# Four weight streams of the mixing layers in three rounded passes, the token shift made while leaving PSUM

## The reference, cut to what matters

```python
for l in range(DEPTH):                       # two mixing layers
    h = _rms_norm(x, norm_pre[l]) * (1 + scale[:, None, :]) + shift[:, None, :]
    p = h @ w_in[l]                          # 256 tokens x 1024, times 1024 x N_IN
...
# RWKV-7 branch: streams holds r, k, v (1024 wide each) and two narrow ones
prev = jnp.pad(streams, ((0, 0), (1, 0), (0, 0)))[:, :-1]
streams = streams + mu * (prev - streams)    # the token shift
r, k, v, w_l, a_l = _split(streams, ...)
w = -jax.nn.softplus(-(w0 + jnp.tanh(w_l) @ w2)) - 0.5
decay = jnp.exp(-jnp.exp(w))
a = jax.nn.sigmoid(a0 + a_l @ a2)
kk = heads(k * k_k)
kk = kk / jnp.maximum(jnp.sqrt(jnp.sum(kk * kk, -1, keepdims=True)), 1e-12)
k = k * (1 + (a - 1) * k_a)
...                                          # state over the tokens, in chunks of 64 here
y = (y - mean) * lax.rsqrt(var + RWKV_GN_EPS)
y = y * ln_w + ln_b
bonus = jnp.sum(r_h * k_h * r_k, -1, keepdims=True) * v_h
o_rwkv = ((y + bonus) * jax.nn.silu(z)) @ w_o
# GLA branch: q, k (512 wide each), v, a gate, z
log_a = jax.nn.log_sigmoid(g_l @ w2 + g_bias) / GLA_GATE_NORM
```

## Time and profile before

| | us |
|---|---|
| median of three runs (2013.95 to 2016.42) | 2014.83 |
| the profiled execution | 2014.74 |
| its span, first to last instruction | 2013.0 |
| TensorE busy | 1929.2 (96%) |
| VectorE busy | 1328.2 (66%) |
| ScalarE busy | 713.8 (35%) |

### The profile page before, as it was taken

How to read it: one execution, slowest core, us unless ns; L and a number is a source line. 1 busy time by engine, 2 the same in 40 slices (tenths; PEclk the granted TensorE clock), 3 DMA queues, 4 the chain that set the end, 5 groups by cost and what they waited for, 6 DMA issues and landing times.

```text
span 2013.0 us, 41616 instructions
## 1 busy us (share of the span) xinstructions
PE 1929.2 (96%) x18047; PEld 1783.3 (89%) x18047; DVE 1328.2 (66%) x1722; ACT 713.8 (35%) x1023; POOL 97.7 (5%) x137
## 2 busy tenths in 40 slices
PE   8999999999899999999999999997999998999998
PEld 8988999998599999989887879996998887888997
DVE  7896687747657866864675339676764676428765
ACT  5573433435533331240423123243222234204243
POOL 2000000100400000020000000001002000000000
PEclk9999999999999998999999999998999999999999
DMA  8555478853347794645440236454653540135643
GB/s 216 140 144 157 149 236 266 266 147 116 99 148 258 253 258 106 166 117 154 118 116 6 74 102 173 122 161 104 170 160 102 148 128 22 45 99 147 164 121 111
DMA packets 473063, 291.41 MB, mean 145 GB/s; under 512 B 26679, under 2 KB 467484, under 8 KB 472776
## 3 DMA queue, kind: packets, MB, share of 16 engines
q1 hardware_dynamic: 466688, 262.20, 46.7%
q0 software_dynamic: 5312, 25.32, 3.3%
q10 hardware_dynamic: 904, 1.58, 0.3%
HBM read 288.02 MB, written 1.05 MB: 144 GB/s over the span
## 4 chain that ended last, share of the span: by engine, by line
PE 82%; DVE 13%; ACT 3%; issue 2%; POOL 0%; DMA 0%; DVEq 0%; ACTq 0%; POOLq 0%
PE bank L705 38%; PE bank L1422 6%; PE bank L1424 6%; PE bank L1423 6%; PE bank L694 4%; PE bank L664 2%; DVE rounded L730 2%; PE bank L901 2%; PE bank L893 2%; PE bank L1625 1%; PE bank L1612 1%; PE bank L1068 1%; PE bank L787 1%; PE bank L1474 1%; PE bank L1593 1%
## 5 line engine op out<-in xcount | busy, mean ns | idle before, releaser
L705 PE MATMUL bank<-rounded 128*128 128x256 f32 (+1 forms) x4584 | 564.2, 284 | 12.0 <-DVE rounded L730 9.4
L705 PEld LDWEIGHTS bank<-rounded 128*128 128x128 f32 (+1 forms) x4584 | 550.6, 189 | 21.2 <-DVE rounded L730 14.6
L730 DVE TENSOR_TENSOR rounded<-arena,rounded 128x1024 fp32r<-128x1024 f32 (+1 forms) x251 | 303.4, 1214 | 86.6 <-ACT rounded L719 80.5
L1422 PE MATMUL bank<-parts 128*128 128x256 f32 x1024 | 290.5, 284 | 1.0 <-DVE parts L2226 1.0
L1424 PE MATMUL bank<-parts 128*128 128x256 f32 x1024 | 289.8, 283 | 0.0
L1423 PE MATMUL bank<-parts 128*128 128x256 f32 x1024 | 289.8, 283 | 0.0
L705 PE MATMUL bank<-common,arena 128*128 128x256 f32 x1280 | 285.4, 380 | 0.0
L705 PEld LDWEIGHTS bank<-common,arena 128*128 128x128 f32 x1280 | 240.1, 189 | 39.8 <-issue 4.8
L770 ACT ACTIVATE arena<-bank 128x512 f32<-128x512 f32 x114 | 67.6, 597 | 436.1 <-PE bank L705 423.1
L1422 PEld LDWEIGHTS bank<-parts 128*128 128x128 f32 x1024 | 196.5, 192 | 1.5 <-issue 1.3
L1423 PEld LDWEIGHTS bank<-parts 128*128 128x128 f32 x1024 | 196.6, 192 | 0.1
(11 more groups left out here) (391 smaller groups left out, 2497.9 us busy)
## 6 DMA issues: line engine op xcount, KB each, us to landing
arena<-in_w_in SPq DMA_DIRECT2D x190, 512.0 KB, 3.8
whole<-in_ffn_w_gate_up SPq DMA_DIRECT2D x44, 1024.0 KB, 5.2
arena<-in_ada_w POOLq DMA_DIRECT2D x32, 768.0 KB, 6.3
whole<-in_ffn_w_down SPq DMA_DIRECT2D x16, 1408.0 KB, 7.0
arena<-in_rec_w_in SPq DMA_DIRECT2D x36, 512.0 KB, 3.8
arena<-in_att_w_qkv SPq DMA_DIRECT2D x24, 512.0 KB, 3.7
arena<-in_rec_w_out SPq DMA_DIRECT2D x16, 512.0 KB, 3.7
arena<-in_mla_w_o SPq DMA_DIRECT2D x16, 512.0 KB, 3.8
```

The costliest lines, as they stand in the source:

```text
L705: last = pe.matmul(psum[s][0:c, m % 2 * T:m % 2 * T + T], w[a][:, k, cols], x[b][:, k, :], start=(k, a, b) == (0, 0, 0), stop=k == job.kt ...
L730: dve.tensor_tensor(raw_view(job_of[u], u, UNIT_LOW), raw, high_view(job_of[u], u).bitcast(F32), ALU.subtract)\
L1422: pe.matmul(bank, w_hi, x_hi, start=start and k == 0, stop=False)
```

## The change

It does the following.

- r, v, gq and gk become split streams, with high parts by ScalarE (24 units in each of the two layers). The high parts of r and v lie in three new buffers, `KEY_HIGHS`; `AA` and `CC` move onto `KKDD` and `V_`, so that `HX` stays as it is until the chunks.
- The token shift of k, r and v is made in two steps. ScalarE leaves PSUM with four reads of 128 x 256 for each bank, where it made one of 128 x 512: each tile times `1 - mu` into the result, and times `mu` into the shifted buffer. VectorE adds the two (`mix_kept_v`), one addition of 2048 numbers a row in place of the subtraction and eight multiply-adds.
- `split_v` is called at eighteen more places of `rwkv_v`, `high_act` at more places of ScalarE's lists.
- The eight multiply-adds by `ln_w` and `ln_b` move from VectorE to ScalarE.
- `HX` is made again right after the last tile of the chunks, not during ro.
- TensorE makes five units of v, not four, ahead of the sums over heads of `RK`, and waits for `HX` ahead of gq, not of gv.

```diff
-        AA, SW, CC = (buf(DK, T) for _ in range(3))
+        SW = buf(DK, T)
+        assert place[0] <= lent + HIGHS * UNIT
+        AA, CC = KKDD, V_
...
-                "k": proj("k", 4, "vector"), "r": proj("r", 4), "v": proj("v", 4),
+                "k": proj("k", 4, "vector"), "r": proj("r", 4, "scalar", highs=KEY_HIGHS), "v": proj("v", 4, "scalar", highs=KEY_HIGHS),
...
-                "gq": proj("gq", 2), "gk": proj("gk", 2),
+                "gq": proj("gq", 2, "scalar"), "gk": proj("gk", 2, "scalar"),
...
-            multiply_units(j["v"], range(4))
+            multiply_units(j["v"], range(5))
             head_sums_pe(RK, DK, abanks)
-            multiply_units(j["v"], range(4, 8))
+            multiply_units(j["v"], range(5, 8))
...
-        def mix_v(src, dst, nt, mu, l):
...
+        def mix_kept_v(shifted, dst):
+
+            dve.tensor_tensor(dst, dst, shifted[:, :, 0:T], ALU.add)\
+               .then_inc(vector_step.sem, 1)
...
             tile_out_v(1)
+            dve.wait_ge(layer_high_again.sem, layer_high_again.due(dve))
+            dve.tensor_tensor(HX[1], H, HX[0].bitcast(F32), ALU.subtract)\
+               .then_inc(layer_split.sem, 1)
...
+            dve.tensor_scalar(KEPT, col(n2("rwkv_mu"), 0, 24), -1.0, 1.0, ALU.mult, ALU.add)\
...
             chunk_tiles_v()
+            split_v(j["gq"].first + 2)
...
+            split_v(j["gk"].first)
             dve.wait_ge(head_rms.sem, head_rms.due(dve))
             dve.tensor_tensor(R, R, RST, ALU.mult)\
...
+               .then_inc(heads_scaled.sem, 1)
+            dve.wait_ge(heads_scaled.sem, heads_scaled.due(dve))
+            split_v(j["gk"].first + 2)
+            dve.wait_ge(heads_shifted.sem, heads_shifted.due(dve, DK))
             dve.tensor_tensor(R, R, BONUS, ALU.add)\
...
+            split_v(j["gk"].through())
             dve.tensor_tensor(R, R, ZR, ALU.mult)\
...
+        def keep_mixed(dst, shifted, mu, l):
+
+            def step(i, bank, done, rounds):
+                for n in range(2):
+                    k = 2 * i + n
+                    act.activation(dst[:, k, :], bank[:, n, :], ACT.Copy, scale=KEPT[:, mu + k:mu + k + 1])\
+                       .then_inc(scalar_step.sem, 1)
+                    scalar_step.due(act)
+                    last = act.activation(shifted[:, k, 1:T + 1], bank[:, n, :], ACT.Copy, scale=col(f"rwkv_mu_2/{l}", mu + k))
+                last.then_inc(done, 1)
+            return step
...
-            take_units(act, j["k"], keep(raw[0], ACT.Copy, 1))
+            take_units(act, j["k"], keep_mixed(KR_, raw[0], 8, l), only=range(3))
+            high_act(j["r"].first)
+            take_units(act, j["k"], keep_mixed(KR_, raw[0], 8, l), only=range(3, 4))
+            high_act(j["r"].first + 2)
...
-            take_units(act, j["r"], keep(raw[1], ACT.Copy, 1))
+            take_units(act, j["r"], keep_mixed(R, raw[1], 0, l), high_before(j["r"], 2))
...
+            act.wait_ge(inner_summed.sem, 2 * l + 2)
+            act.activation(HX[0], H, ACT.Copy)\
+               .then_inc(layer_high_again.sem, 1)
+            high_act(j["gq"].first + 2)
+            take_units(act, j["rz2"], keep(ZR[:, 6:], ACT.Silu))
...
-            take_units(act, j["gq"], keep(GQ, ACT.Copy))
-            take_units(act, j["gk"], keep(GK, ACT.Copy), high_before(j["gk"], 4), only=range(1))
+            take_units(act, j["gq"], keep(GQ, ACT.Copy), high_before(j["gq"], 2), only=range(1))
+            high_act(j["gk"].first + 1)
+            act.wait_ge(heads_scaled.sem, heads_scaled.due(act))
+            for k in range(DK):
+                act.activation(R[:, k, :], R[:, k, :], ACT.Identity, bias=col(f"rwkv_ln_b_2/{l}", k), scale=col(f"rwkv_ln_w_2/{l}", k))\
+                   .then_inc(heads_shifted.sem, 1)
+            take_units(act, j["gq"], keep(GQ, ACT.Copy), only=range(1, 2))
+            take_units(act, j["gk"], keep(GK, ACT.Copy), high_before(j["gk"], 2), only=range(1))
             act.wait_ge(gate_in.sem, gate_in.due(act))
...
-            take_units(act, j["gk"], keep(GK, ACT.Copy), high_before(j["gk"], 3), only=range(1, 2))
+            take_units(act, j["gk"], keep(GK, ACT.Copy), high_before(j["gk"], 2), only=range(1, 2))
             high_act(j["ro"].first + 3)
```

More of the change, by code:

```diff
@@ L397, in program @@
         ECEND = buf(DK, 4)
-        KAI = buf(8)
+        KAI, KEPT = buf(8), buf(24)
         assert place[0] <= AR
         place[0] = after_preparation
+        KEY_HIGHS = [rounded(UNIT, at=aligned() + n * UNIT) for n in range(HIGHS)]
         R_HIGH = rounded(DK, T)
@@ L2778, in rwkv_v @@
             dve.wait_ge(cumulated.sem, cumulated.due(dve))
+            split_v(j["r"].first + 4)
             dve.tensor_scalar(KAI, col(n2("rwkv_k_a"), 0, 8), -1.0, 1.0, ALU.mult, ALU.add)\
@@ L2788, in rwkv_v @@
             dve.wait_ge(vector_step.sem, kfactors)
+            split_v(j["r"].first + 5)
             dve.tensor_tensor(KR_, KR_, KFACTOR, ALU.mult)\
@@ L2791, in rwkv_v @@
             dve.wait_ge(vector_step.sem, vector_step.due(dve))
+            split_v(j["v"].first)
             for k in range(0, DK, 2):
@@ L2804, in rwkv_v @@
             dve.wait_ge(vector_step.sem, vector_step.due(dve))
+            split_v(j["v"].first + 3)
             dve.tensor_tensor(RK, RK, along(col(n2("rwkv_r_k"), 0, 8), DK, T), ALU.mult)\
@@ L2807, in rwkv_v @@
             dve.wait_ge(head_squares.sem, head_squares.due(dve))
+            split_v(j["v"].first + 4)
             dve.wait_ge(head_rms.sem, head_rms.due(dve))
@@ L2811, in rwkv_v @@
             dve.wait_ge(vector_step.sem, vector_step.due(dve))
+            split_v(j["v"].first + 5)
             dve.tensor_tensor(BDF, KKD, AA, ALU.mult)\
@@ L2814, in rwkv_v @@
             dve.wait_ge(vector_step.sem, vector_step.due(dve))
+            split_v(j["v"].first + 6)
             dve.wait_ge(decays.sem, decays.due(dve))
@@ L2821, in rwkv_v @@
             dve.wait_ge(vector_step.sem, vector_step.due(dve))
+            split_v(j["v"].through())
             dve.tensor_tensor(BDF, BDF, E2, ALU.mult)\
@@ L3378, in rwkv_act @@
             act.wait_ge(scalar_step.sem, scalar_step.due(act))
+            high_act(j["v"].first + 4)
             act.activation(flat(SW), flat(SW), ACT.Exp, scale=-KAPPA)\
@@ L3381, in rwkv_act @@
             act.wait_ge(decays.sem, decays.due(act))
+            take_units(act, j["v"], keep_mixed(V_, raw[2], 16, l), only=range(1))
             act.wait_ge(guarded_squares.sem, guarded_squares.due(act))
@@ L3385, in rwkv_act @@
             act.wait_ge(scalar_step.sem, scalar_step.due(act))
+            high_act(j["v"].first + 5)
             act.activation(flat(SQR), flat(SQR), ACT.Exp, scale=-0.5)\
@@ L3388, in rwkv_act @@
             act.wait_ge(head_rms.sem, head_rms.due(act))
-            take_units(act, j["v"], keep(raw[2], ACT.Copy, 1), only=range(2))
+            take_units(act, j["v"], keep_mixed(V_, raw[2], 16, l), only=range(1, 2))
+            high_act(j["v"].first + 6)
             for k in range(0, DK, 2):
@@ L3396, in rwkv_act @@
                 act.nop().then_inc(bonus_sums.sem, 1)
-            take_units(act, j["v"], keep(raw[2], ACT.Copy, 1), only=range(2, 4))
+            high_act(j["v"].through())
+            take_units(act, j["v"], keep_mixed(V_, raw[2], 16, l), only=range(2, 4))
             act.wait_ge(taken[0].sem, halves(0, j["mo"]))
```

46 lines of the change are left out of this document (18 added, 28 removed).

## The result

The changed kernel takes **2037.05 us** (median of 4 runs, 2035.79 to 2038.55), the one before, run beside it, 2014.67. The ratio is 1.0109, 95% interval 1.0097 to 1.0122: 22 us slower, where the prediction said 30. The profiled execution has a span of 2034.0 us against 2013.0.

What follows compares the result with a forecast made beforehand. TensorE was taken to set the pace in both stretches. Added waits less savings, 0.2 + 3.0 + 12.1 = 15.3 us a layer, twice 30.6, on a median of 2014.83 gave 2045 us; range 2037 to 2050 (70%).

Steps and rivals of the forecast that it cites:

- k to r: Between k and r: ScalarE's longer bank reads and two high parts delay the gates; r begins 3.55 us later.
- lost in r: During r: TensorE waits for VectorE's low parts of units 4, 5 and 6, together 3.2 us.
- lost in v and head sums: During v: waits for low parts 1.5, sums of `RK` 1.4, unit 7 2.8; together 5.7 us.
- wait of the R sums: After the chunks: low part of `HX` and three low parts stand ahead of the head sums' signal, 0.9 us.
- gq unit 3: In gq: unit 3's high part queues on ScalarE behind the exponential of the norms; TensorE waits 2.8 us.
- waits in gk: In gk: its two last high parts follow weight and bias on ScalarE; waits of 1.4 and 0.7 us.
- pause ahead of ro: Between gk and ro: ro's first high parts stand behind the gate's exponential and logarithm; TensorE waits 10.5 us.
- ro to gv: During ro: one wait of 2.1 us, gate sums ahead of unit 2, against 1.6 before; +0.5.
- L1713 to gv: Stretch behind the chunks: waits less the saving on gq and gk sum to +12.1 us a layer.
- Rival 3: Ahead of ro and at the gates: TensorE's clock falls after new pauses, up to 2.4 us each; 2055 at most, 14%.
- Rival 2: Ahead of ro: only this wait is small, so 10.5 us a layer go; 2024 us, chance 10%.
- Rival 1: All split streams: VectorE's low parts ready in time everywhere, all 28.2 us gained; 1986.5 us, chance 6%.

Runs made afterwards that it cites:

- head: gates_first, with VectorE's low parts of r and of v's last unit also moved earlier in its list: 2024.56 us, ratio 1.0048.
- both2: head and tail, plus the gate's input made earlier in SQT's space and more of ro's parts ahead of the gate work: 1997.51 us, ratio 0.9916.
- ro_ahead: Changed kernel with ro's first two high parts and their low parts moved ahead of the gate on ScalarE and VectorE: 2039.89 us, ratio 1.0131.
- both: Changed kernel with the reorderings of head and tail together: 2016.88 us, ratio 1.0006.
- filled: Changed kernel with 16 useless matmuls put into TensorE's pause ahead of ro: 2038.51 us, ratio 1.0121.
- tail: Changed kernel with only the stretch behind the chunks reordered, some of gq's and ro's parts made earlier: 2031.80 us, ratio 1.0082.
- gates_first: Changed kernel with no high copy between k's last bank and the gates on ScalarE: 2033.75 us, ratio 1.0097.

## Why the prediction was right, and 8 us high, by its steps

First layer, us:

| step | predicted | measured |
|---|---|---|
| k to r | +3.75 (0.2 of it in k) | +3.81 |
| lost in r | 3.2 | 2.7 (listed waits 0.84, 0.96, 0.36; the rest to eight units at 2.88) |
| lost in v and head sums | 5.7 | 4.4, of it 2.7 ahead of unit 7 |
| saved on r and v | 9.4 | 9.4 |
| sum to the chunks | +3.2 | +1.6 (second layer +3.0) |
| wait of the R sums (the first head sums behind the chunks) | 0.9 | 0 (L1713 to the head sums 9.05 in both kernels) |
| gq unit 3 | 2.8 | 2.76, and 1.5 of half clock |
| waits in gk | 2.1 | 0 |
| pause ahead of ro | 10.5 | 8.8 |
| ro to gv | +0.5 | +0.3 |
| saved on gq and gk | 4.7 | 4.2, as what the other rows leave |
| L1713 to gv | +12.1 | +9.2 (second layer +8.9) |

**Right:** the sign, the places, and what ends each wait. "ro's first high parts stand behind the gate's exponential and logarithm" is the chain above, row by row; TensorE waits for VectorE's low parts in r and v, 5.6 us where the prediction said about 8, and unit 7 stands where said. One wait was not there: the head sums of `RK` run through in 3.03 us, as the others do. ScalarE came to their banks at 1016.89, not 1019.7, so the 1.4 us at the fourth bank never came.

**A sign of being wrong that showed:** VectorE was to have no idle time while TensorE works through r and v. It stood idle 2.52, 1.15, 3.37 and 2.39 us there, waiting for ScalarE (L3397, L723, L3418) and TensorE (L897). The forecast tells only of the first of these waits. A unit is late by the place of its low part in VectorE's list, not only because VectorE has too much to do: head moves nothing but high and low parts, and the 2.69 us ahead of unit 7 became 0.36.

**Mis-sized**, all in one direction, on VectorE's and ScalarE's side:
- *A scaled read out of PSUM at 0.507 each, 2.03 a bank.* They came at 0.36, 1.44 a bank: my cheap bound was 1.6. The 0.507 was the pitch of sigmoids of which each waits for the one before. ScalarE at k's last bank, the reads (L3367, L3370) and the table load with the first sigmoid:

```profile
958.61 0.47 ACT L3367 ACTIVATE arena<-bank,arena 128x256 f32<-128x256 f32 x1 [3.25 <-PE bank L709]
958.98 0.47 ACT L3370 ACTIVATE arena<-bank,common 128x256 f32<-128x256 f32 x1
...
962.08 1.28 ACT L3391 ACT_TABLE_LOAD   x1
963.38 0.47 ACT L3391 ACTIVATE arena<-bank,common 128x256 f32<-128x256 f32 x1
```

  The Trainium skill, page "ScalarE: Activation LUTs", section "What ACT_TABLE_LOAD costs", gives the overlap of ACTIVATEs back to back as about 93 ns; an estimate from it is 0.47 less that, 0.38. The trace agrees to 0.02 us, and the price was to be had. The first sigmoid came 28.76 us behind k's start, forecast 29.2; the half clock on the products behind it took that back.
- *A low part 1.24.* Followed by work that doesn't need it, it costs 1.14: three in a row took 3.49 us (L734 from 1177.08).
- *Weight and bias 5.0.* Eight took 4.05 in a row (L3511 from 1202.95). I took the upper end, by the row nearest in form; the cheap bound 0.5 each was right.
- With these VectorE was ahead at the R sums and at gk, so that 0.9 + 2.1 us of waits never came, and ro was ready earlier.

**Rival 3** was not a case beside the forecast but part of what happened: the clock fell in each layer at three to four places. I had put its price, up to 2.4 us for each, on TensorE alone. Measured, it is nothing behind the chunks of the changed kernel, 1.25 us a layer there in head, and up to 2.5 us a layer ahead of the chunks from one execution to another. **Rival 2** (only ro's pause small) fell: the pause was 8.8 us. **Rival 1** is the instructive one. At 6% it was right to doubt it for the change as written, since product and low part take 3.5 us against 2.88. Its rule, to relieve the engine with the highest occupancy, failed for this order; with another order of the same operations, and another place for the gate's input, 17 of its 28 us came (both2).

## What to carry to other kernels

A split that saves TensorE 0.585 us a unit costs VectorE 1.14 and ScalarE 1.06; whether it pays is decided by where those two stand in their queues, unit by unit. Read the chain across engines ahead of the pause, and repair all of it: moving its first link alone gained nothing (ro_ahead, 1.0131 against 1.0109, with gv 1.6 us later), moving everything but the last link gave nothing over before (both). Look for buffers that overlay: GX and GE over ZR, not a need for data, kept the gate behind the branch.

## What the runs showed of the hardware

- TensorE's clock fell to 0.50 to 0.61 also after pauses of 1.86 (filled), 2.22 (tail) and 3.25 us (the gates of the changed kernel), on the work that had resumed; in the pause of 8.77 us it was at 0.50 already while TensorE stood still. Pauses of 1.36 (gates_first), 1.64 (both2) and 2.12 us (gates_first) were followed by 1.00. The same wait ahead of v's last unit, 2.69 and 2.68 us, was followed by full clock in one layer of the changed kernel and by half in the other.
- A table load took 1.28 us, and the next ACTIVATE began 0.02 us behind its end.
- A scaled Copy of 128x256 out of PSUM lasts 0.47 us and repeats at 0.36; a wait for each on the one before makes it 0.507.
